# Pairs of expert blocks by seven block products in the second half of a dense expert sum

## The chip, the cores and the metric

The kernel runs on one core of a Trainium2 chip. Its time is the device time of one launch in microseconds (us), the median of several runs. PE is TensorE, DVE is VectorE, ACT is ScalarE, POOL is GpSimd, SP is SyncE.

## What is computed

Two transformer blocks, one behind the other, on 256 tokens of width 2048, in float32. The change is in the last stage of the second block, the expert layer:

```
        expert = jnp.take_along_axis(cand_i, pos, axis=-1)
        g = jax.nn.softmax(top_s, axis=-1)
        u = u_emb[expert]
        a = jax.nn.gelu(jnp.einsum('thkd,td->thk', u, xb).astype(jnp.float32), approximate=False)
        coef = (g * a).astype(xb.dtype)
        return jnp.einsum('thk,thkd->td', coef, v_emb[expert])
```

There are 128 x 128 experts. A token chooses 128 of them (8 heads, 16 each). The result is added to the residual and normalised.

## The kernel before

The expert layer is computed densely. A stage U multiplies all 16384 rows of `peer_u` with the tokens, and a gate table, zero where a token did not choose an expert, makes the coefficients `G[:, j, :]` (128 experts of block j by 256 tokens). Stage V is one product: coefficients, transposed, times `peer_v`, summed over 128 blocks j. It goes in two halves of the output's columns: for c = 0 all blocks j and columns 0 to 1023, then for c = 1 all blocks j and columns 1024 to 2047. `PLAN` lists these tiles in order; tile ("V", j, c) is a load of 128 x 1024 (512 KB) and 12 matmuls.

Every float32 product is made of three matmuls (`three`, lines 940 to 943): high by high, high by low and low by high. The high part of an operand is a copy rounded by ACT, the low part is a subtraction on DVE (raw minus high). So each tile needs: the load into `raw` (SP's queue, four buffers, line 842; it waits for the low part of the tile four before), ACT's `cut` (line 2273, three buffers `wh`), DVE's `cut` (line 1481, into `wl`), and the coefficients' high part on ACT (`coef_high`, line 2655) and low part on DVE (`coef_low`, line 2189), two buffers. In the iteration of tile j, ACT and DVE make the coefficients of tile j + 1 and cut the weights of the tile two further on. Both wait, through ACT, for the end of tile j - 1 on PE. PE (`v_tile`) waits for the low weights and the low coefficients of its tile, and adds into four PSUM banks (two of 128 tokens by two of 512 columns) over all j. Each engine has its own list of instructions, in the order in which the code is written, and runs it in that order; between engines there are semaphores only.

Columns 0 to 1023 stay in PSUM banks 4 to 7 until they are added to the residual, which comes back from memory (`PIECE`, line 918) into `fin` and is summed, squared and scaled at tiles 50 to 64 (`ADD_AT`). The last tiles and the end of the norm stand behind. GpSimd does nothing in this stage; its sums of 128x256 and 128x258 in earlier stages are at lines 2721 and 2759.

## Time and profile before

| | |
|---|---|
| median of 3 runs | 3175.16 us (3174.51 to 3175.98) |
| profiled execution | 3175.95 us, its span 3174.1 us |
| busy share of the span | PE 100%, PE's weight loads 95%, DVE 66%, ACT 57%, POOL 14% |
| traffic | 627.77 MB, mean 198 GB/s |

Busy time counts from an instruction's start to its end. Matmuls are pipelined and overlap, so the duration of one is more than what it adds to the time. An instruction on DVE or ACT can also start a little before the one ahead has ended.

### The profile page before, as it was taken

To read this page: it belongs to the slowest core of one execution; us is meant where nothing else is said; L and a number is where in the kernel's file an instruction comes from. 1 tells how busy PE (TensorE), PEld (TensorE's weight loads), DVE (VectorE), ACT (ScalarE), POOL (GpSimd) and SP (SyncE) were. 2 spreads that over 40 slices of the span, in tenths; PEclk is the share of its full clock that TensorE was granted. 3 is DMA by queue.
4 is the path that set the end of the run, shared out by engine and by line. 5 is a ranking of instruction groups with operands and counts; after the bars stand their busy time and mean duration, and the time that the engine had idled before them with its cause. 6 is when DMAs were issued, how large, how long until landed. Compare 5 with 4: busy or idle time off the path is not lost.

```text
span 3174.1 us, 58774 instructions
## 1 busy us (share of the span) xinstructions
PE 3160.3 (100%) x24186; PEld 3018.3 (95%) x24186; DVE 2096.0 (66%) x3389; ACT 1804.0 (57%) x2580; POOL 458.0 (14%) x321
## 2 busy tenths in 40 slices
PE   9999999999999999999999999999999999999998
PEld 9999999999999999999999999999999888888887
DVE  7987486666664477665666699855555666666665
ACT  6566464444444455545455578877777544555545
POOL 0001200000000000000000056777760000000000
PEclk9999999999999999999999999999999999999999
DMA  6444557666666656545565577888876777766555
GB/s 224 151 146 134 183 181 235 225 226 229 226 201 194 194 172 206 163 153 166 187 196 197 199 190 194 196 195 195 194 195 196 243 242 242 242 226 216 195 194 168
DMA packets 229419, 627.77 MB, mean 198 GB/s; under 512 B 59328, under 2 KB 78624, under 8 KB 229024
## 3 DMA queue, kind: packets, MB, share of 16 engines
q1 hardware_dynamic: 192144, 623.60, 60.7%
q0 software_dynamic: 36864, 0.15, 3.3%
q8 instruction: 192, 3.15, 0.4%
q14 instruction: 75, 0.61, 0.1%
q10 hardware_dynamic: 144, 0.26, 0.0%
HBM read 601.27 MB, written 21.10 MB: 196 GB/s over the span
## 4 chain that ended last, share of the span: by engine, by line
PE 98%; DVE 1%; ACT 0%; DMA 0%; issue 0%; POOL 0%; SPq 0%; DVEq 0%; ACTq 0%; POOLq 0%
PE ps L941 32%; PE ps L942 31%; PE ps L943 31%; PE ps L1014 0%; DVE wl L1481 0%; PE ps L1215 0%; PE ps L1238 0%; PE ps L1235 0%; PE ps L982 0%; DMA raw<-in_in1k 0%; PE ps L1411 0%; PE ps L1249 0%; PE ps L1239 0%; PE ps L1067 0%; PE ps L1016 0%
## 5 line engine op out<-in xcount | busy, mean ns | idle before, releaser
L2273 ACT CAST wh<-raw 128x1024 fp32r<-128x1024 f32 (+3 forms) x1114 | 1158.2, 1040 | 1029.7 <-PE ps L943 1008.4
L1481 DVE TENSOR_TENSOR wl<-raw,wh 128x1024 fp32r<-128x1024 f32 (+2 forms) x883 | 1061.8, 1203 | 407.8 <-ACT wh L2273 405.4
L941 PE MATMUL ps<-xh,wh 128*128 128x256 f32 x3088 | 854.7, 277 | 0.5 <-issue 0.5
L943 PE MATMUL ps<-xh,wl 128*128 128x256 f32 x3088 | 850.0, 275 | 0.0
L942 PE MATMUL ps<-xl,wh 128*128 128x256 f32 x3088 | 849.8, 275 | 0.0
L941 PE MATMUL ps<-xw,wh 128*128 128x258 f32 (+2 forms) x2096 | 591.7, 282 | 2.8 <-DVE wl L1542 1.7
L943 PE MATMUL ps<-xw,wl 128*128 128x258 f32 (+2 forms) x2096 | 587.6, 280 | 0.0
L941 PEld LDWEIGHTS ps<-xh,wh 128*128 128x128 f32 x3088 | 579.7, 188 | 4.3 <-issue 1.6
L942 PEld LDWEIGHTS ps<-xl,wh 128*128 128x128 f32 x3088 | 579.8, 188 | 1.1 <-issue 1.0
L943 PEld LDWEIGHTS ps<-xh,wl 128*128 128x128 f32 x3088 | 579.6, 188 | 0.0
L2784 POOL DMA_INDIRECT table<-w_loose x256 | 397.6, 1553 | 809.3 <-DVE w_loose L2161 656.3
L1481 DVE TENSOR_TENSOR wl<-raw,ph 128x1024 fp32r<-128x1024 f32 x231 | 281.2, 1220 | 224.4 <-ACT ph L2278 187.7
L942 PE MATMUL ps<-xw,wh 128*128 128x258 f32 (+2 forms) x1441 | 404.2, 281 | 0.0
L941 PEld LDWEIGHTS ps<-xw,wh 128*128 128x128 f32 x2096 | 394.3, 188 | 5.4 <-DVE wl L1542 2.1
L943 PE MATMUL ps<-wh,coefs 128*128 128x512 f32 x1020 | 396.8, 389 | 0.0
L941 PE MATMUL ps<-wh,coefs 128*128 128x512 f32 x1020 | 396.8, 389 | 0.0
L942 PE MATMUL ps<-wl,coefs 128*128 128x512 f32 x1020 | 396.8, 389 | 0.0
L943 PEld LDWEIGHTS ps<-xw,wl 128*128 128x128 f32 x2096 | 394.0, 188 | 0.0
L942 PEld LDWEIGHTS ps<-xw,wh 128*128 128x128 f32 x1441 | 270.8, 188 | 0.1
L2278 ACT CAST ph<-raw 128x1024 fp32r<-128x1024 f32 x231 | 232.7, 1007 | 0.0
L941 PEld LDWEIGHTS ps<-wh,coefs 128*128 128x128 f32 x1020 | 191.4, 188 | 39.8
L943 PEld LDWEIGHTS ps<-wh,coefs 128*128 128x128 f32 x1020 | 191.4, 188 | 39.8
(398 smaller groups left out, 4454.7 us busy)
## 6 DMA issues: line engine op xcount, KB each, us to landing
raw<-in_peer_u SPq DMA_DIRECT2D x256, 512.0 KB
raw<-in_peer_v SPq DMA_DIRECT2D x256, 512.0 KB
...
```

The lines of the kernel that those rows point to most:

```text
L941: t.matmul(o, lh, rh, start=start, stop=False)
L942: t.matmul(o, lh, rl, start=False, stop=False)
L943: return t.matmul(o, ll, rh, start=False, stop=stop)
L1481: v.tensor_tensor(part_at(wl, i), raw[:, i % RN, 0:cols(i)], high.bitcast(F32), ALU.subtract).then_inc(lo, 1)
L2273: last = s.copy(part_at(wh, i), raw[:, i % RN, 0:cols(i)])
L2278: last = s.copy(ph[:, 2 + i % 2, :], raw[:, i % RN, 0:cols(i)])
L2784: g.indirect_dma_start(out=table, out_offset=bass.IndirectOffsetOnAxis(ap=eidx[q][:, n:n + 1], axis=0), in_=wts[q][:, n:n + 1], in_offset= ...
```

## The change

In the second half (c = 1), eleven pairs of neighbouring blocks (26 and 27, 34 and 35, ... 106 and 107) leave the plan of tiles. A pair is a 2 x 2 by 2 x 2 block product: coefficients of two blocks for two groups of tokens, times weights of two blocks for two groups of columns. Eight block products of three matmuls (24) become seven (21), in the manner of Strassen and Winograd: some factors are sums of blocks, and the results go to the four banks of this half and to four more, which collect over all pairs and are folded in once behind the last.

A pair's rows are loaded apart, into columns of `G` that are no longer needed. GpSimd makes four sums of 128x512 (weights) and four of 128x128 (coefficients) in the six tiles between two pairs (`pair_sums`). ACT makes the high parts (`pair_step` of the scalar part) and DVE the low parts (`pair_low_of`) in five steps of 512, 1024, 1024, 1024 and 512 columns, one to a tile (`BEHIND_PAIR`); the low part is written over the raw sum. PE (`v_pair`) computes the pair ahead of tile j + 2. The load of the next pair stands in SP's queue ahead of a tile's load and waits for DVE's second step and GpSimd's fourth sum of the pair before, which are the last readers of these rows. The residual's first half is added at tiles 11 to 14, as banks 4 to 7 are wanted by the pairs. The lines left out of the diff write `fin` as a function `fin_at` with another layout, and fold the extra banks in (`fold`, eight sums at tiles 109 to 116).

```diff
@@ -158,7 +158,10 @@
 PLAN += [("out2", m, c) for m in range(16) for c in range(2)]
 PLAN += [("wq", m, c) for m in range(8) for c in range(2)]
 PLAN += [("U", j, c) for j in range(128) for c in range(2)]
-PLAN += [("V", j, c) for c in range(2) for j in range(128)]
+PAIRS = [26 + 8 * n for n in range(11)]
+PAIRED = [j + e for j in PAIRS for e in range(2)]
+SINGLE = [j for j in range(128) if j not in PAIRED]
+PLAN += [("V", j, 0) for j in range(128)] + [("V", j, 1) for j in SINGLE]
 AT = {key: i for i, key in enumerate(PLAN)}
 NCH = len(PLAN)
 I1, O1, GU, DN = AT["in1k", 0, 0], AT["out1", 0, 0], AT["guk", 0, 0], AT["down", 0, 0]
@@ -166,9 +169,17 @@
 I2, BA, O2, WQ, U0 = AT["in2k", 0, 0], AT["ba", 0, 0], AT["out2", 0, 0], AT["wq", 0, 0], AT["U", 0, 0]
 V1 = AT["V", 0, 1]
 
-PIECE = {AT["V", 10 + 2 * n, 1]: n for n in range(12)}
-
-ADD_AT = [50 + 4 * n for n in range(4)]
+PIECE = {AT["V", j, 1]: n for n, j in enumerate((8, 10, 12, 14, 109, 110, 111, 112, 28, 30, 32, 33))}
+
+ADD_AT = [11, 12, 13, 14]
+SQUARE_AT, GAIN_AT = [113, 114, 115, 116], [117, 118, 119, 120]
+
+
+BETWEEN = PAIRS[1] - PAIRS[0] - 2
+PAIR_LOAD = {AT["V", 20, 1]: 0}
+PAIR_LOAD.update({AT["V", j - BETWEEN, 1] + 9: n + 1 for n, j in enumerate(PAIRS[:-1])})
+BEHIND_PAIR = {j - BETWEEN + o: (n, o) for n, j in enumerate(PAIRS) for o in range(BETWEEN)}
+FOLD = {PAIRS[-1] + 3 + n: n for n in range(8)}
 UEND = [AT["U", j, 1] - U0 for j in range(128)]
 UAT = {slot + 1: j for j, slot in enumerate(UEND)}
 
...
+    def fin_at(qt, c, n=512):
+        o = 2 * CH * (c // CH) + CH * qt + c % CH
+        return flatG[:, o:o + n]
+
+    pair_high, pair_low = [x[:, PAD_X[3]:PAD_X[3] + KT * S] for x in xbuf]
+    pair_raw = x_loose[:, 1, PAD_X[3]:PAD_X[3] + KT * S]
+    B11, B21, B22, T1_, T3_, T2_, T4_, SUMS = range(8)
...
+    RAW11, RAW12, RAW21, RAW22 = [flatG[:, 2 * CH + 512 * n:2 * CH + 512 * n + 512] for n in range(4)]
+    RAW_ROWS = flatG[:, 3 * CH:4 * CH]
+    folded = flatG[:, 3 * D + 3 * CH:3 * D + 3 * CH + 512]
...
@@ -914,10 +943,24 @@
                     y.wait_ge(d_spill, 16)
                 y.wait_ge(c_l, 128 + 2 * n + 2)
                 c = slice(512 * (n % 4), 512 * (n % 4) + 512)
+                if n == 4:
+                    y.wait_ge(pair_lo, PAIR_LO + 5 * (len(PAIRS) - 1) + 2)
+                    y.wait_ge(pair_sum, PAIR_SUM + 8 * (len(PAIRS) - 1) + 4)
                 if n < 8:
-                    y.dma_start(fin[:, n // 4, c], spill[:, n // 4, c]).then_inc(d_re, 16)
+                    qt, x = n // 2 % 2, CH * (n // 4) + 512 * (n % 2)
+                    y.dma_start(fin_at(qt, x), spill[:, qt, x:x + 512]).then_inc(d_re if n < 4 else d_gf, 16)
                 else:
                     y.dma_start(gain[:, c], A["g_final"][:, c]).then_inc(d_gf, 16)
+            if i in PAIR_LOAD:
+                n = PAIR_LOAD[i]
+                if n:
+                    y.wait_ge(pair_lo, PAIR_LO + 5 * (n - 1) + 2)
+                    y.wait_ge(pair_sum, PAIR_SUM + 8 * (n - 1) + 4)
+                else:
+                    y.wait_ge(c_l, 128 + 16)
+                for e in range(2):
+                    j = PAIRS[n] + e
+                    y.dma_start(flatG[:, (2 + e) * CH:(3 + e) * CH], A["peer_v_2"][128 * j:128 * j + 128, CH:2 * CH]).then_inc(d_pair, 16)
             load(i)
             if 0 <= i - I2 - 6 < len(SIDES2):
                 for name, a in SIDES2[i - I2 - 6]:
@@ -1433,6 +1476,34 @@
                 last = v_part_of(j, half, a)
             last.then_inc(gemm, 1)
 
+        def v_pair(n):
+            j = PAIRS[n]
+            one, two = 128 + j, 128 + j + 1
+            first, last = n == 0, n == len(PAIRS) - 1
+
+            def product(o, left, b, start, stop):
+                return three(o[:], *left, pair_block(pair_high, b), pair_block(pair_low, b), start, stop)
+
+            def single(tile, qt):
+                tk = slice(128 * qt, 128 * qt + 128)
+                return coef_at(0, tile)[:, tk], coef_at(1, tile)[:, tk]
+
+            def summed(i):
+                return pair_sum_at(pair_high, i), pair_sum_at(pair_low, i)
+
+            if first:
+                t.wait_ge(f_add, 4)
+            t.wait_ge(pair_lo, PAIR_LO + 5 * (n + 1))
+            t.wait_ge(c_l, one + 1)
+            product(ps[4], single(one, 0), B11, first, last)
+            product(ps[5], summed(0), T1_, first, last)
+            t.wait_ge(c_l, two + 1)
+            product(acc(1, 0, 0), single(two, 0), B21, False, False)
+            product(acc(1, 1, 0), single(two, 1), T4_, False, False).then_inc(pair_mm, 1)
+            product(acc(1, 0, 1), summed(3), B22, False, False)
+            product(ps[6], summed(1), T2_, first, last)
+            product(ps[7], summed(2), T3_, first, last).then_inc(pair_mm, 1)
+
         def v_last():
 
             for j in range(125, 128):
@@ -1462,6 +1533,8 @@
             elif (j, c) == (125, 1):
                 v_last()
             elif c == 0 or j < 125:
+                if c and j - 2 in PAIRS:
+                    v_pair(PAIRS.index(j - 2))
                 v_tile(j, c)
             if i < V1:
                 for step, a in SIDES3[i - U0]:
...
+            x = fin_at(qt, 512 * i)
             v.tensor_tensor(x, x, acc(half, qt, b)[:], ALU.add).then_inc(f_add, 1)
 
+        def pair_step(n, o):
+            if 1 <= o < 6:
+                pair_low_of(n, o - 1)
+
+        def pair_low_of(n, q):
+            x, y = ((0, 512), (512, 1536), (1536, 2560), (2560, 3584), (3584, 4096))[q]
+            whole_ = RAW11 if q == 0 else RAW_ROWS if q == 1 else pair_raw[:, x:y]
+            v.wait_ge(pair_hi, PAIR_HI + 5 * n + q + 1)
+            v.tensor_tensor(pair_low[:, x:y], whole_, pair_high[:, x:y].bitcast(F32), ALU.subtract).then_inc(pair_lo, 1)
+
+        def fold(n):
+
+            steps = [(folded, ps[4]), (fin_at(0, CH + 512), folded), (fin_at(0, CH + 512), ps[5]), (folded, ps[7]),
+                     (fin_at(1, CH), folded), (fin_at(1, CH + 512), folded), (fin_at(1, CH + 512), ps[5]), (fin_at(0, CH), ps[4])]
+            x, y = steps[n]
+            if n == 0:
+                v.wait_ge(pair_hi, PAIR_HI + 5 * len(PAIRS) + 1)
+                v.wait_ge(d_gf, 16 * 8)
+            else:
+                v.wait_ge(pair_sum, PAIR_SUM + 8 * len(PAIRS) + n)
...
+            v.tensor_tensor(x, x, y if y is folded else y[:], ALU.add).then_inc(pair_sum, 1)
+
         for j in range(128):
+            if j in PAIRS:
+                coef_low(128 + j + 1)
+                cut(AT["V", j + 2, 1] + 2)
+                continue
             if j < 125:
                 coef_low(128 + j + 1)
             if j == 124:
@@ -2220,18 +2319,22 @@
                     last = v.tensor_tensor(part_at(wl, NCH - 1)[:, c], raw[:, (NCH - 1) % RN, c],
                                            part_at(wh, NCH - 1)[:, c].bitcast(F32), ALU.subtract)
                 last.then_inc(lo, 1)
-            else:
-                cut(V1 + j + 2)
+            elif j in SINGLE and j - 2 not in PAIRS:
+                cut(AT["V", j, 1] + 2)
+            if j in BEHIND_PAIR:
+                pair_step(*BEHIND_PAIR[j])
+            if j in FOLD:
+                fold(FOLD[j])
             if j in ADD_AT:
                 n = ADD_AT.index(j)
                 if n == 0:
-                    v.wait_ge(d_re, 16 * 8)
...
@@ -2648,6 +2751,8 @@
             j = n % 128
             if n == 255:
                 s.wait_ge(gemm, AT["U", 127, 1] + 1)
+            elif n >= 130 and n - 130 in PAIRED:
+                s.wait_ge(pair_mm, PAIR_MM + 2 * (PAIRED.index(n - 130) // 2) + 1)
             elif n >= 2:
                 s.wait_ge(gemm, AT["V", (n - 2) % 128, (n - 2) // 128] + 1)
+            s.activation(squares[:, qt, 512 * i:512 * i + 512], fin_at(qt, 512 * i), ACT.Square,
                          accum_out=ssum[:, qt, i:i + 1]).then_inc(f_sq, 1)
 
+        def pair_step(n, o):
+            if o > 4:
+                return
+            x, y = ((0, 512), (512, 1536), (1536, 2560), (2560, 3584), (3584, 4096))[o]
+            whole_ = RAW11 if o == 0 else RAW_ROWS if o == 1 else pair_raw[:, x:y]
+            if o == 0:
+                if n:
+                    s.wait_ge(pair_mm, PAIR_MM + 2 * n)
+                s.wait_ge(d_pair, D_PAIR + 32 * (n + 1))
+            elif o > 1:
+                s.wait_ge(pair_sum, PAIR_SUM + 8 * n + (3, 4, 8)[o - 2])
+            s.copy(pair_high[:, x:y], whole_).then_inc(pair_hi, 1)
+
         for j in range(128):
+            if j in PAIRS:
+                coef_high(128 + j + 1)
+                cut(AT["V", j + 2, 1] + 2)
+                continue
             if j < 126:
                 coef_high(128 + j + 1)
             if j == 124:
@@ -2682,10 +2804,15 @@
                 s.wait_ge(gemm, i - SN + 1)
                 s.copy(part_at(wh, i)[:, 0:512], raw[:, i % RN, 0:512]).then_inc(hi_front, 1)
                 s.copy(part_at(wh, i)[:, 512:CH], raw[:, i % RN, 512:CH]).then_inc(hi, 1)
-            else:
+            elif j in SINGLE and j - 2 not in PAIRS:
                 cut(AT["V", j, 1] + 2)
-            if j - 1 in ADD_AT:
-                n = ADD_AT.index(j - 1)
+            if j in BEHIND_PAIR:
+                pair_step(*BEHIND_PAIR[j])
+            if j == PAIRS[-1] + 2:
+                s.wait_ge(pair_mm, PAIR_MM + 2 * len(PAIRS))
+                s.copy(folded, ps[6][:]).then_inc(pair_hi, 1)
+            if j in SQUARE_AT:
+                n = SQUARE_AT.index(j)
                 square_up(0, n // 2, n % 2)
         for qt in range(2):
...
+
+        def pair_sums(n):
+            j = PAIRS[n]
+            g.wait_ge(coef, j + 2)
+            g.wait_ge(c_l, 128 + 16)
+            a11, a21, a12, a22 = [G[:, j + e, 128 * qt:128 * qt + 128] for e in range(2) for qt in range(2)]
+            t1, t2, t3, t4 = [pair_block(pair_raw, b) for b in (T1_, T2_, T3_, T4_)]
+            sums = [pair_sum_at(pair_raw, i) for i in range(4)]
+            done = PAIR_SUM + 8 * n
+            if n:
+                g.wait_ge(pair_mm, PAIR_MM + 2 * n)
+            g.wait_ge(d_pair, D_PAIR + 32 * (n + 1))
+            g.tensor_tensor(t1, RAW12, RAW11, ALU.subtract).then_inc(pair_sum, 1)
+            g.tensor_tensor(t3, RAW22, RAW12, ALU.subtract).then_inc(pair_sum, 1)
+            g.wait_ge(pair_sum, done + 1)
+            g.tensor_tensor(t2, RAW22, t1, ALU.subtract).then_inc(pair_sum, 1)
+            g.wait_ge(pair_sum, done + 3)
+            g.tensor_tensor(t4, RAW21, t2, ALU.subtract).then_inc(pair_sum, 1)
+            g.tensor_tensor(sums[0], a21, a22, ALU.add).then_inc(pair_sum, 1)
+            g.tensor_tensor(sums[2], a11, a21, ALU.subtract).then_inc(pair_sum, 1)
+            g.wait_ge(pair_sum, done + 5)
+            g.tensor_tensor(sums[1], sums[0], a11, ALU.subtract).then_inc(pair_sum, 1)
+            g.wait_ge(pair_sum, done + 7)
+            g.tensor_tensor(sums[3], a12, sums[1], ALU.subtract).then_inc(pair_sum, 1)
+
+        for n in range(len(PAIRS)):
+            pair_sums(n)
 
     px.close()
     top.close()
```

How the instructions stand now. On DVE, in the second half of V before, two kinds of rows alternate from tile to tile (`coefs` is `coef_low`, `wl` the cut of the weights):

```order
L2189 TENSOR_TENSOR coefs<-G,coefs 128x256
L1481 TENSOR_TENSOR wl<-raw,wh 128x1024
L2189 TENSOR_TENSOR coefs<-G,coefs 128x256
L1481 TENSOR_TENSOR wl<-raw,wh 128x1024
L2189 TENSOR_TENSOR coefs<-G,coefs 128x256
```

In the changed kernel the same place, from the last four steps ahead of one pair to the first cut behind it (`xl` is the pair's low part, L2262 is `coef_low` and L1554 the cut):

```order
L2290 TENSOR_TENSOR xl<-x_loose,xh 128x1024
L2262 TENSOR_TENSOR coefs<-G,coefs 128x256
L1554 TENSOR_TENSOR wl<-raw,wh 128x1024
L2290 TENSOR_TENSOR xl<-x_loose,xh 128x512
L2262 TENSOR_TENSOR coefs<-G,coefs 128x256
L1554 TENSOR_TENSOR wl<-raw,wh 128x1024
L2262 TENSOR_TENSOR coefs<-G,coefs 128x256 x3
L1554 TENSOR_TENSOR wl<-raw,wh 128x1024
```

Each tile between two pairs has a third instruction behind its cut, and the pair's last piece (512 columns) stands behind the cut of a tile that comes after the pair. On GpSimd, which had no row in this stage, one pair's sums read (`x_loose` is the pair's raw buffer):

```order
L2945 TENSOR_TENSOR x_loose<-G 128x512
L2946 TENSOR_TENSOR x_loose<-G 128x512
L2948 TENSOR_TENSOR x_loose<-G,x_loose 128x512
L2950 TENSOR_TENSOR x_loose<-G,x_loose 128x512
L2951 TENSOR_TENSOR x_loose<-G 128x128
L2952 TENSOR_TENSOR x_loose<-G 128x128
L2954 TENSOR_TENSOR x_loose<-x_loose,G 128x128
L2956 TENSOR_TENSOR x_loose<-G,x_loose 128x128
```

Both inputs of every one lie in SBUF, as do both inputs of DVE's coefficients, cuts and pieces.

## Rows read from the trace of the kernel before

**Rows 1.** The page: busy us (share) x instructions; granted clock in tenths, 40 slices.

```profile
PE 3160.3 (100%) x24186; PEld 3018.3 (95%) x24186; DVE 2096.0 (66%) x3389; ACT 1804.0 (57%) x2580; POOL 458.0 (14%) x321
...
PEclk9999999999999999999999999999999999999999
```

**Rows 2.** The page: the chain that ended last, by engine.

```profile
PE 98%; DVE 1%; ACT 0%; DMA 0%; issue 0%; POOL 0%; SPq 0%; DVEq 0%; ACTq 0%; POOLq 0%
```

**Rows 3.** Windows of V, halves 1 and 2: busy us, clock, DMA share, GB/s.

```profile
2500.00:2600.00 100.00, 100.00 (x443) 82.81 (x442) 69.54 (x110) 49.55 (x74) 0.00 (x0) 1.00 0.75 241
...
2810.00:3155.00 345.00, 345.00 (x1524) 285.67 (x1523) 213.81 (x263) 175.01 (x263) 0.00 (x0) 1.00 0.62 201
```

**Rows 4.** Timeline, second half of V: start, us, engine, line [idle before].

```profile
2901.74 0.39 PE L941 MATMUL ps<-wh,coefs 128*128 128x512 f32 x1
...
2901.94 0.41 ACT L2655 CAST coefs<-G 128x256 fp32r<-128x256 f32 x1 [1.36 <-PE ps L943]
...
2902.25 1.05 ACT L2273 CAST wh<-raw 128x1024 fp32r<-128x1024 f32 x1
2902.38 0.43 DVE L2189 TENSOR_TENSOR coefs<-G,coefs 128x256 fp32r<-128x256 f32 x1 [0.54 <-ACT coefs L2655]
...
2903.34 1.23 DVE L1481 TENSOR_TENSOR wl<-raw,wh 128x1024 fp32r<-128x1024 f32 x1 [0.53 <-ACT wh L2273]
...
2904.46 0.39 PE L941 MATMUL ps<-wh,coefs 128*128 128x512 f32 x1
```

**Rows 5.** Timeline, DVE: two cuts back to back, merged.

```profile
932.82 2.35 DVE L1481 TENSOR_TENSOR wl<-raw,wh 128x1024 fp32r<-128x1024 f32 x2
```

**Rows 6.** Groups by form: busy us, mean ns of one.

```profile
L1481 DVE TENSOR_TENSOR wl<-raw,wh 128x512 fp32r<-128x512 f32 x16 | 11.1, 693 | 17.0 <-ACT wh L2273 17.0
...
L1835 DVE SCALAR_TENSOR_TENSOR snt<-mt,snt 128x768 f32<-128x768 f32 x1 | 1.0, 954 | 0.0
...
L2273 ACT CAST wh<-raw 128x512 fp32r<-128x512 f32 x16 | 10.0, 622 | 26.6 <-PE ps L943 26.6
```

**Rows 7.** Timeline at the start: PE released by DVE.

```profile
9.30 0.69 DVE L1542 TENSOR_TENSOR wl<-raw,wh 128x512 fp32r<-128x512 f32 x1 [1.73 <-ACT wh L2315]
...
10.04 0.39 PE L941 MATMUL ps<-xw,wh 128*128 128x272 f32 x1 [1.20 <-DVE wl L1542]
...
10.27 0.28 PE L942 MATMUL ps<-xw,wh 128*128 128x272 f32 x1
```

**Rows 8.** Timeline: a GpSimd sum just ahead of a DVE instruction.

```profile
931.34 0.74 POOL L2721 TENSOR_TENSOR tmp<-tmp 128x256 f32<-128x256 f32 x1 [481.18 <-ACT tmp L2437]
...
931.38 1.52 DVE L1833 SCALAR_TENSOR_TENSOR snt<-mt 128x768 f32<-128x768 f32 x1
```

**Rows 9.** Timeline: a GpSimd sum issued during a cut on DVE.

```profile
946.29 1.22 DVE L1481 TENSOR_TENSOR wl<-raw,wh 128x1024 fp32r<-128x1024 f32 x1 [0.46 <-ACT wh L2273]
...
946.62 1.50 POOL L2721 TENSOR_TENSOR tmp<-tmp 128x256 f32<-128x256 f32 x1 [14.53 <-ACT tmp L2437]
```

**Rows 10.** Groups by form, POOL: fills of one and of 1024 columns.

```profile
L2763 POOL MEMSET tmp<- 128x1024 f32 x1 | 1.0, 956 | 49.6 <-DVE rstd L1515 49.6
...
L2917 POOL MEMSET const-uint8-127<- 128x1 uint8 x1 | 0.1, 129 | 0.0
```

**Rows 11.** DMA issues: KB each, median us from issue to landing.

```profile
spill<-G SPq DMA_DIRECT2D x1, 2048.0 KB, 7.8
G<-spill SPq DMA_DIRECT2D x8, 256.0 KB, 5.2
```

**Rows 12.** Timelines of DVE and POOL: a GpSimd sum across a boundary on DVE.

```profile
114.74 1.21 DVE L1481 TENSOR_TENSOR wl<-raw,wh 128x1024 fp32r<-128x1024 f32 x1
115.87 0.71 DVE L1648 SCALAR_TENSOR_TENSOR pexp<-pexp,stat 16x16 f32<-16x16 f32 x1
...
114.90 1.65 POOL L2759 TENSOR_TENSOR csum<-cacc 128x258 f32<-128x258 f32 x1 [88.48 <-DVE cacc L1692]
...
272.57 1.22 DVE L1481 TENSOR_TENSOR wl<-raw,wh 128x1024 fp32r<-128x1024 f32 x1
...
272.34 2.06 POOL L2759 TENSOR_TENSOR csum<-csum,cacc 128x258 f32<-128x258 f32 x1 [62.96 <-DVE cacc L1692]
```

More of the change, by code:

```diff
@@ L933, in _ @@
                     y.wait_ge(sem, 2 * qt + n + 1)
-                    y.dma_start(out[128 * qt:128 * qt + 128, c:c + 512], fin[:, qt, c:c + 512]).then_inc(d_out, 16)
+                    y.dma_start(out[128 * qt:128 * qt + 128, c:c + 512], fin_at(qt, c)).then_inc(d_out, 16)
         y.wait_ge(d_out, 8 * 16)
@@ L2670, in square_up @@
             s.wait_ge(f_add, n + 1)
-            s.activation(squares[:, qt, 512 * i:512 * i + 512], fin[:, qt, 512 * i:512 * i + 512], ACT.Square,
+            s.activation(squares[:, qt, 512 * i:512 * i + 512], fin_at(qt, 512 * i), ACT.Square,
                          accum_out=ssum[:, qt, i:i + 1]).then_inc(f_sq, 1)
+        def pair_step(n, o):
[10 more added lines that the diff above has]
+            s.copy(pair_high[:, x:y], whole_).then_inc(pair_hi, 1)
         for j in range(128):
+            if j in PAIRS:
+                coef_high(128 + j + 1)
+                cut(AT["V", j + 2, 1] + 2)
+                continue
             if j < 126:
@@ L2697, in _ @@
                     s.wait_ge(f_add, 8 + n)
-                    s.activation(squares[:, 1, c:c + 256], fin[:, 1, c:c + 256], ACT.Square,
+                    s.activation(squares[:, 1, c:c + 256], fin_at(1, c, 256), ACT.Square,
                                  accum_out=ssum[:, 1, 3 + n:4 + n]).then_inc(f_sq, 1)
@@ L2704, in _ @@
             for c in (0, 512):
-                x = fin[:, qt, c:c + 512]
+                x = fin_at(qt, c)
                 s.activation(x, x, ACT.Copy, scale=r).then_inc(f_out, 1)
@@ L2708, in _ @@
                 s.wait_ge(f_out, 4)
-                s.dma_start(out[128:256, 512:1024], fin[:, 1, 512:1024]).then_inc(d_out, 16)
+                s.dma_start(out[128:256, 512:1024], fin_at(1, 512)).then_inc(d_out, 16)
     @block.gpsimd
```

19 lines of the change are left out of this document (12 added, 7 removed).

## The prediction

> **What bounds the kernel now.** I read the busy shares first: PE is busy for the whole span, at the full clock, and POOL has almost nothing to do [rows 1]. The chain of waits says the same from the other end: 98% of it is PE [rows 2]. For the stretch that the change touches, the second half of V, the windows give PE 345.00 busy of 345.00 us, with DVE at 62% and ACT at 51% [rows 3]. So here time is matmuls times their pitch, plus whatever a change makes PE wait. In the timeline one tile's first matmul starts at 2901.74 and the next tile's at 2904.46, 2.72 us later: 12 matmuls, 0.2267 us each [rows 4]. Their own 0.39 us overlap, so that figure is not the price.
>
> The same rows give the rhythm of the helpers, which I count from a tile's first matmul T (2901.74). ACT gets word that the tile before is done at T+0.20 and makes the high coefficients, then the high half of the weights; DVE starts its low coefficients at T+0.64 and its low weights at T+1.60, ending at T+2.83 [rows 4]. Back to back a DVE instruction costs less than its duration, as each starts before the last has ended: two cuts of 1024 take 2.35 us, so 1.13 apiece where one lasts 1.22 [rows 5]. Taking the same 0.09 off, 256 columns cost 0.34, and a cut of 512, which lasts 0.69 (ACT's 0.62), costs 0.60 [rows 6].
>
> **What the change removes.** A pair has 7 products of 3 matmuls in place of two tiles with 12 each: 21 for 24. Eleven pairs drop 33 matmuls, all 512 wide: 33 x 0.2267 = 7.5 us. Nothing else on PE goes away. That is 0.24% of 3175.16, hardly more than the 0.2% that a measurement of this kernel tells from no change, so the waits decide.
>
> **What it adds on DVE and ACT.** Per period of eight tiles two cuts go and 4096 columns of high and low parts come: on DVE 2 x 1.13 less, 0.60 + 3 x 1.13 + 0.60 = 4.59 more. Averages are fine (about 14 us of DVE in 21 us), but the place is not. All of the 4.59 stands in the five tiles ahead of the pair, and the last piece stands behind a cut that cannot come earlier. I set 0 at the first matmul of tile 28, the first behind a pair, and walk DVE to the next pair (34, 35), due at 6 x 2.72 = 16.32:
> - tile 29 (2.72): coefficients 3.36 to 3.70, cut at 4.32 to 5.45, first piece to 6.05
> - tile 30 (5.44): coefficients 6.08 to 6.42, cut at 7.04 to 8.17, second piece to 9.30
> - tile 31: coefficients to 9.64, cut 9.76 to 10.89, third piece to 12.02
> - tile 32: coefficients to 12.36, cut 12.48 to 13.61, fourth piece to 14.74
> - tile 33 (13.60): coefficients to 15.08, cut waits for ACT until 15.20, to 16.33, last piece ends at 16.33 + 0.69 = 17.02.
>
> PE waits for all five pieces before the pair's first product. It is 0.70 late; a stalled PE starts 0.05 after the release, and its second matmul comes 0.23 behind the first, where at 272 columns 0.12 is the pitch (0.2267 x 272 / 512) [rows 7], so each pair costs about 0.85 us. The last cut is for the second tile behind the pair and nobody needs it yet, but it stands ahead of the piece that is needed. Eleven times 0.85 is 9.4 us: with GpSimd costing nothing the sum is already -7.5 + 9.4 = +1.9 us, 3177. ACT (0.41 + 1.05 + 1.05 = 2.5 a tile) fits in 2.72.
>
> **What GpSimd's sums cost.** They are on no chain by themselves, but they read SBUF while DVE does. A 128x256 sum took 0.74 us beside a DVE instruction that came just after it, and that DVE instruction took 1.52 [rows 8], where its like of the same size takes 0.954 [rows 6]: DVE was held 0.57 us, to 0.61 after the sum's start. The other way round, a sum issued 0.33 after a cut took 1.50 and ended 0.61 after the cut [rows 9]. So the two exclude each other, with 0.13 us of dispatch ahead and about 0.48 in which DVE is held. No 512-wide sum is in this trace. Below, the slope of the fills, (956 - 129) / 1023 = 0.81 ns a column, makes it 0.61 + 0.21 = 0.82; above, twice the whole, 1.48 with dispatch. I take 0.10 to 0.13 as fixed, from the one-column fill [rows 10], which leaves 2.0 ns a column, nearest to the sum's own row: 1.12 for 512 (0.99 of it holding DVE), 0.35 for 128 (0.22 holding).
>
> The eight sums start at 0.2, when the pair before has finished. Two of 512 are over before DVE's first work at 3.36. The third, from about 3.1, holds DVE 0.75, the fourth 1.0, the four small ones 0.2 each: 2.55 in all. DVE's waits for ACT in the walk above (0.62 + 0.03 + 0.62 + 3 x 0.12 = 1.63) absorb that much; 0.9 is left. Behind the first pair, whose sums run before DVE is loaded, a pair costs 0.85 + 0.9 = 1.75. Together 0.85 + 10 x 1.75 = 18.4, less 7.5: **+10.9 us, 3186**. The profiled execution took 3175.95, its span 3174.1; both stand within 1 us of the median, so the difference goes on either.
>
> The Trainium skill (SBUF — State Buffer, "Who interferes with whom") has it harder: a DVE instruction with two SBUF inputs and a GpSimd one that reads SBUF exclude each other for the whole instruction. The exclusion agrees with the trace [rows 8, 9]; that DVE was let go 0.13 us before the sum's end does not. By the whole instruction the blocks would be 0.9 + 1.12 + 4 x 0.35 = 3.4 a period, 1.8 left, 2.65 a pair, and the sum +19.9 (3195). The row decides, but it is of 256 columns, so 3195 lies in my range. The same skill (GPSIMD Engine Reference, "Elementwise — side-by-side cycle accounting") gives 4497 ns for such a sum of 2048 columns; no run here shows it, and an estimate between it and the 0.74 row is 1.28 for 512 with dispatch, which would leave the sum where it is.
>
> **What costs nothing.** SP's queue now waits at each pair's loads for DVE's second piece (about 9.3 to 11.4) and the fourth sum (6.8). Behind it stand the loads of tiles 31 and on in the next period, whose first reader comes some 14 us later; the pair's own 1 MB is read at 23.5. Landing took 5.2 us for 256 KB and 7.8 for 2 MB [rows 11], so 12 us cover it. The bytes are the same in nearly the same time, 201 GB/s, and the first half of V ran at 241 without a wait of PE [rows 3]. If the cover went, each late load would stall the pair by what it is late. The added sums at tiles 11 to 14, the eight folds at 109 to 116 (0.68 each behind 0.34 + 1.13, so 2.15 of 2.72) and the squares on ACT fit in their tiles, and the tail after the last matmul is the same instructions.
>
> **The rivals.**
> - *The sums find gaps and DVE loses nothing* (the sums shorter than I take them, below 1.0 us for 512): +2 to +6, 3177 to 3181. For it: DVE pauses four times in a period. Against: DVE is nearly full from 9.30 on. 0.20.
> - *DVE keeps the port from one instruction to the next*, and the sums get in only when it pauses. The rows speak both ways: a sum issued at 114.90 got in at the end of the running cut, and a 16x16 instruction issued behind it took 0.71; one issued at 272.34 ended 2.06 later, 0.61 after a cut that started at 272.57, so it missed the boundary at 272.66 [rows 12]. Behind the last sum stand ACT's 0.62, then coefficients and a cut on ACT (1.4) and coefficients, cut and piece on DVE (0.34 + 1.13 + 0.69), about 4.4 us. It bites once the last sum ends later than 11.9; near 15.8 it makes each later pair 3.9 late: 0.85 + 39 - 7.5 = +32, 3207. 0.13.
> - *Faster*: the pair starts unhindered. The one place is the last piece: if it ended by 16.3 at every pair, the 7.5 us would stand, 3167.7. It needs the last cut to be 0.7 us shorter or earlier, and the rows fix all its terms [rows 4 to 6]; it decides below 0.1 us of stall a pair. 0.04.
> - *Stalls bring PE's clock down* from 2.4 to 1.2 GHz, of which no row of V shows anything (granted 1.00, also at the start with 1.2 us stalls). Then a stretch behind each pair would cost double, far over 3207. 0.02.
>
> **How the numbers follow.** My forecast (+7 to +22, with the alternation of DVE and GpSimd) has 0.61, 3182 to 3197 by itself. The range runs from the floor, 3177, to 3206, which leaves out the faster case, the clock and part of the port rival: about 0.17. The same case below +6.3 us: 0.20. Faster 0.04. Slower 0.76.
>
> **What would show it.** PE's busy time loses 7.5 us of matmul while the span grows; waits of PE's first product of a pair on DVE's low pieces, eleven, the first near 0.8 and the others near 1.7; DVE's coefficients and pieces with 0.2 to 1.0 us added while a GpSimd sum of 512 runs, and none of the 4.6 us of pieces missing. Granted clock 1.00. I am wrong if the pieces are over before the pair is due, if the waits fall on loads, or if the sums leave DVE's durations alone.

## The result: 3195.8 us, 0.65% slower

After the change the kernel takes 3195.81 us (median; 3195.35 to 3196.55, 4 runs) beside 3175.11 of the kernel before: a ratio of 1.0065, 95% interval 1.0053 to 1.0078. The profiled execution has a span of 3194.7 us, 20.6 more than before. Slower was the likeliest case and the time lies in the range, but the size is nearly twice the +10.9 us that the prediction had. One execution of the kernel of experiment 12 went at a granted clock of 0.83 and took 3558.41 us; it is left out, and all others used here went at 0.998 or more. The page of after, beside [rows 1, 2]: busy us and share of each engine, the granted clock in tenths, and the chain of waits by engine.

```profile
PE 3167.6 (99%) x24153; PEld 3012.0 (94%) x24153; DVE 2147.8 (67%) x3430; ACT 1825.9 (57%) x2614; POOL 560.7 (18%) x409
...
PEclk9999999999999999999999999999999999999999
...
PE 93%; DVE 6%; ACT 1%; DMA 0%; issue 0%; POOL 0%; SPq 0%; DVEq 0%; ACTq 0%; POOLq 0%
```

The prediction wanted PE's busy time to lose 7.5 us. 33 matmuls are gone, and yet it gained 7.3. The waits (engine, line, releaser: us in total, times, longest) show stalls on both of DVE's products:

```profile
PE ps L984 <- DVE xl L2290: 11.5, 10, 2.3
...
PE ps L984 <- DVE coefs L2262: 0.8, 3, 0.4
```

A wait that the profile puts down to nobody is missing there, so I measured stalls by the starts of neighbouring matmuls instead. After's timeline in one period: DVE and POOL behind a pair, then the next pair's start (start, us, engine, line).

```profile
2920.76 1.30 POOL L2948 TENSOR_TENSOR x_loose<-G,x_loose 128x512 f32<-128x512 f32 x1
2921.30 1.04 DVE L2262 TENSOR_TENSOR coefs<-G,coefs 128x256 fp32r<-128x256 f32 x1 [4.12 <-ACT coefs L2760]
2922.14 1.36 POOL L2950 TENSOR_TENSOR x_loose<-G,x_loose 128x512 f32<-128x512 f32 x1
2922.27 2.32 DVE L1554 TENSOR_TENSOR wl<-raw,wh 128x1024 fp32r<-128x1024 f32 x1
...
2934.33 1.21 DVE L1554 TENSOR_TENSOR wl<-raw,wh 128x1024 fp32r<-128x1024 f32 x1
...
2934.78 0.39 PE L986 MATMUL ps<-wh,coefs 128*128 128x512 f32 x1
...
2935.47 0.68 DVE L2290 TENSOR_TENSOR xl<-x_loose,xh 128x512 fp32r<-128x512 f32 x1
...
2936.20 0.49 PE L984 MATMUL ps<-xh,coefs 128*128 128x512 f32 x1 [1.03 <-DVE xl L2290]
2936.54 0.39 PE L985 MATMUL ps<-xl,coefs 128*128 128x512 f32 x1
```

Both mechanisms of the forecast are there. The last piece stands behind a cut and releases PE at 2936.15 (2935.47 + 0.68); 1.42 us lie between the pair's first matmul and the one before it, and 0.34 behind it. And a cut that takes 1.22 alone took 2.32, since GpSimd's fourth sum ran until 2923.50: the cut ended 1.09 us later, so DVE was let go 0.13 before the sum's end. The same 0.13 comes out at the coefficients (1.04 for 0.41, 0.28 after the third sum's end at 2922.06).

What was not foreseen is between the stalls. In this piece of after nothing waits; the first row and the one 12 matmuls behind it:

```profile
2999.83 0.40 PE L986 MATMUL ps<-wh,coefs 128*128 128x512 f32 x1
...
3002.63 0.40 PE L986 MATMUL ps<-wh,coefs 128*128 128x512 f32 x1
```

That is 2.80 us for 12, 0.2333 apiece, where before has 2.72 and 0.2267 [rows 4], with the granted clock at 1.00 in both. I call this distance from one matmul's start to the next one's the pitch. From the first stall (2868.35) up to 3150 us, after has 72 stretches of 13 gaps in which nothing stalls: 68 go at 0.2333 and 4 lie between the two values; in before, all 95 such stretches go at 0.2267. There are some 1,140 gaps between 2868.35 and 3154, and what they take above 0.2267, stalls apart, is 7.3 us.

The second surprise is at the last pair. ScalarE waits for two tiles that SP's queue issued late: in front of them, at the first of the residual's late pieces (line 948), the queue itself had waited 14.0 us. PE stalls 2.4 us, and the granted clock falls. The wait of SP's queue (engine, line, releaser: us in total, times, longest):

```profile
SPq L948 <- DVE xl L2290: 14.0, 1, 14.0
```

After's timeline, ScalarE and PE:

```profile
3120.98 1.05 ACT L2376 CAST wh<-raw 128x1024 fp32r<-128x1024 f32 x1 [1.64 <-DMA raw<-in_peer_v]
...
3123.94 0.79 PE L984 MATMUL ps<-xh,coefs 128*128 128x512 f32 x1 [2.25 <-DVE xl L2290]
3124.53 0.63 PE L985 MATMUL ps<-xl,coefs 128*128 128x512 f32 x1
3124.96 0.63 PE L986 MATMUL ps<-xh,coefs 128*128 128x512 f32 x1
```

The matmuls behind the wait are 0.43 us apart. The windows of after for that stretch (us; busy of PE, PEld, DVE, ACT, POOL with their counts; clock, DMA share, GB/s) have the clock at 0.52, most of the time at the lower of its two levels:

```profile
3123.50:3127.00 3.50, 3.06 (x7) 2.48 (x8) 1.95 (x3) 1.04 (x1) 0.00 (x0) 0.52 1.02 397
```

The sum of after, from its own timeline: the gaps between matmuls, each less 0.2333, come to 20.55 us (first pair with the tiles ahead of it 1.5, nine regular pairs at 1.63 = 14.7, last pair 4.3), plus 7.3 for the pitch, less 7.5: +20.4, where 20.6 was measured.

### The profile page after: what moved, and what is told of

Its sections match the earlier page's. It is cut to its first block, busy times and chain, and to the rows that moved or that the text cites. A ratio compares the mean times of both kernels' runs of the same rounds, so it can differ in the third digit from the quotient of the medians.

```text
span 3194.7 us, 58881 instructions
## 1 busy us (share of the span) xinstructions
PE 3167.6 (99%) x24153; PEld 3012.0 (94%) x24153; DVE 2147.8 (67%) x3430; ACT 1825.9 (57%) x2614; POOL 560.7 (18%) x409
## 4 chain that ended last, share of the span: by engine, by line
PE 93%; DVE 6%; ACT 1%; DMA 0%; issue 0%; POOL 0%; SPq 0%; DVEq 0%; ACTq 0%; POOLq 0%
PE ps L984 30%; PE ps L985 30%; PE ps L986 30%; DVE wl L1554 2%; DVE xl L2290 2%; DVE coefs L2262 1%; PE ps L1057 0%; PE ps L1258 0%; PE ps L1278 0%; PE ps L1281 0%; PE ps L1025 0%; PE ps L1454 0%; PE ps L1292 0%; PE ps L1282 0%; DMA raw<-in_peer_v 0%
## 5 line engine op out<-in xcount | busy, mean ns | idle before, releaser
L2376 ACT CAST wh<-raw 128x1024 fp32r<-128x1024 f32 (+3 forms) x1092 | 1134.8, 1039 | 1032.2 <-PE ps L986 1009.5
L1554 DVE TENSOR_TENSOR wl<-raw,wh 128x1024 fp32r<-128x1024 f32 (+2 forms) x861 | 1050.4, 1221 | 364.4 <-ACT wh L2376 360.5
L1554 DVE TENSOR_TENSOR wl<-raw,ph 128x1024 fp32r<-128x1024 f32 x231 | 281.2, 1220 | 224.0 <-ACT ph L2381 203.0
L984 PE MATMUL ps<-wh,coefs 128*128 128x512 f32 x932 | 366.0, 393 | 1.7 <-DVE coefs L2262 0.8
L985 PE MATMUL ps<-wl,coefs 128*128 128x512 f32 x932 | 364.6, 391 | 0.0
L986 PE MATMUL ps<-wh,coefs 128*128 128x512 f32 x932 | 364.5, 391 | 0.0
L2262 DVE TENSOR_TENSOR coefs<-G,coefs 128x256 fp32r<-128x256 f32 x254 | 118.0, 468 | 183.5 <-ACT coefs L2760 183.2
L984 PEld LDWEIGHTS ps<-wh,coefs 128*128 128x128 f32 x932 | 175.1, 188 | 44.8 <-issue 8.1
```

The costliest lines, as they stand in the source:

```text
L984: t.matmul(o, lh, rh, start=start, stop=False)
L985: t.matmul(o, lh, rl, start=False, stop=False)
L986: return t.matmul(o, ll, rh, start=False, stop=stop)
L1554: v.tensor_tensor(part_at(wl, i), raw[:, i % RN, 0:cols(i)], high.bitcast(F32), ALU.subtract).then_inc(lo, 1)
L2262: v.tensor_tensor(coef_at(1, n), G[:, n % 128, :], coef_at(0, n).bitcast(F32), ALU.subtract).then_inc(c_l, 1)
L2376: last = s.copy(part_at(wh, i), raw[:, i % RN, 0:cols(i)])
```

## The experiments

Twelve kernels, each timed beside the kernel before (3175.3 to 3175.6 us on those chips). Times are medians; "stalls" are the gaps between matmuls summed as above, and "stretches" are 13 gaps without a stall, from 2868 to 3150 us.

**1. One short wait in the kernel before.** Nothing of the change is in it.

```diff
             t.wait_ge(c_l, n + 1)
+            if n == 128 + 20:
+                t.wait_ge(lo, AT["V", 21, 1] + 1)
```

> The kernel before with one extra wait: PE starts tile 20 of the second half only when the low weights of tile 21 are done, which stalls it once, by about 0.2 us. Theory (a stall of PE in V leaves the matmul pitch at 0.2333 us instead of 0.2267 for all that follows): 108 tiles x 12 x 0.0066 = 8.5 us more, about 3184. Rival (the longer pitch comes from the pairs, from GpSimd or from the other work): 0.2 us more, 3175.3, pitch 0.2267 to the end.

3183.96 us, ratio 1.0028 [1.0018, 1.0038]. Its timeline around the wait:

```profile
2869.16 0.39 PE L942 MATMUL ps<-wl,coefs 128*128 128x512 f32 x1
...
2870.52 0.39 PE L942 MATMUL ps<-wl,coefs 128*128 128x512 f32 x1
2870.74 0.39 PE L943 MATMUL ps<-wh,coefs 128*128 128x512 f32 x1
2871.22 0.47 PE L941 MATMUL ps<-wh,coefs 128*128 128x512 f32 x1
2871.52 0.40 PE L942 MATMUL ps<-wl,coefs 128*128 128x512 f32 x1
...
2874.32 0.40 PE L942 MATMUL ps<-wl,coefs 128*128 128x512 f32 x1
```

From 2869.16 to 2870.52 there are 6 matmuls, 0.2267 apiece; 0.48 and 0.30 at it, a stall of 0.3 us; then 2871.52 to 2874.32 for 12, and so to the end. A stall of 0.3 us cost 8.7: the time moved as the theory had it, and not by the rival's 0.2.

**2 to 4. The parts of the stalls.** Run 2 puts fills of the same places for GpSimd's sums (its result and run 4's lack them); run 3 puts DVE's last piece ahead of the cut; run 4 does both.

```diff
-            g.tensor_tensor(t1, RAW12, RAW11, ALU.subtract).then_inc(pair_sum, 1)
+            g.memset(t1, 0.0).then_inc(pair_sum, 1)
...
             elif j in SINGLE and j - 2 not in PAIRS:
+                if BEHIND_PAIR.get(j, (0, 0))[1] == 5:
+                    pair_step(*BEHIND_PAIR[j])
                 cut(AT["V", j, 1] + 2)
```

> The changed kernel with GpSimd's eight sums a pair replaced by fills of the same tiles with zero (the sums are left out): the same order and semaphores, but nothing is read. Theory (a sum that reads SBUF holds DVE, and DVE it): DVE's coefficients, cuts and pieces keep 0.42, 1.22 and 0.69, each pair waits 0.85 instead of 1.65, so about 8 us less, 3188. Rival (GpSimd's sums are too slow or the held DVE does not matter): 3195 to 3196.

> The changed kernel with DVE's last piece of a pair ahead of the cut of the tile behind the pair instead of behind it. Theory (the place behind that cut is 1.1 us of each pair's wait): the wait falls from about 1.2 to 0.1 to 0.2 us at eleven pairs, some 11 us less, 3184 to 3185. Rival (the cut becomes late instead): a wait of the same size on the low weights, 3195.

> Both at once: fills in place of sums (sums left out) and the last piece first. Theory (the stalls, and the pitch that they leave behind, are all that stands against the 33 matmuls): no wait of PE between the pairs, pitch 0.2267 to the end, 3175.1 - 7.5 = 3167.7. Rival (pairs cost something by themselves, or the pitch changes without a stall): 3176 or more.

Run 2: 3184.06, ratio 1.0028 [1.0017, 1.0039]; stalls 9.1 us. A cut's mean is 1226 ns again (after: 1421), PE's waits for the pieces are half, and a pair costs 0.78 us where the walk had 0.85. Grouped by line between 2870 and 3150 us, after and then run 2:

```profile
L1554 DVE TENSOR_TENSOR wl<-raw,wh 128x1024 fp32r<-128x1024 f32 x75 | 106.5, 1421 | 8.0 <-ACT wh L2376 6.6
```

```profile
L1554 DVE TENSOR_TENSOR wl<-raw,wh 128x1024 fp32r<-128x1024 f32 x79 | 96.9, 1226 | 29.2 <-ACT wh L2376 26.2
```

Run 2's waits of PE, for the 11.5 of after:

```profile
PE ps L984 <- DVE xl L2290: 5.6, 10, 1.0
```

Run 3: 3182.58, ratio 1.0022 [1.0013, 1.0032]; stalls 7.1 us, 3.9 of them now at a tile's coefficients, 0.3 and more apiece, and 3.2 at the pairs. Either edit takes 12 to 13 us off after, more than the 8 and 11 expected: the 20.55 us of stalls fell by 11.4 and 13.4, the long last one among them. Run 4: 3175.50, ratio 1.0001 [0.9991, 1.0010]. It stalls nowhere, no weights load of PE comes late at the first pair or ahead of it, and its pitch still goes to 0.2333 at the first pair. I had expected 3167.7. So a stall is not the only thing that changes the pitch.

**5. The late residual.** SP's queue asks for the second half's residual behind tiles 111 to 114 instead of 109 to 112; folds and gains move back with it.

```diff
-PIECE = {... (8, 10, 12, 14, 109, 110, 111, 112, 28, 30, 32, 33))}
+PIECE = {... (8, 10, 12, 14, 111, 112, 113, 114, 28, 30, 32, 33))}
-FOLD = {PAIRS[-1] + 3 + n: n for n in range(8)}
+FOLD = {PAIRS[-1] + 6 + n: n for n in range(8)}
```

> After's kernel with the four late residual pieces asked for behind tiles 111 to 114 instead of 109 to 112, and the folds three tiles and the gains three tiles later. In after's trace ScalarE waits 1.64 and 1.56 us for a raw tile just ahead of the last pair, the pair is 2.6 us late instead of 1.4, and the granted clock is 0.5 for 3.4 us behind it. Theory (the residual pieces' waits at the head of SP's queue delay the loads of tiles 109 and 110): ScalarE's two waits are gone, the last pair stalls like the others, the clock stays at 1.00, and the time is 2.7 to 3 us below after's, about 3193. Rival (the last pair is late for another reason): still 3195.8 with the low clock.

3193.48, ratio 1.0057 [1.0040, 1.0074]: 2.3 us below after, where 2.7 to 3 were expected; stalls 17.5. ScalarE's waits for raw tiles and the queue's 14.0 us are gone, the last pair stalls like the others, and the clock is 1.00 in the windows:

```profile
3100.00:3130.00 30.00, 28.86 (x124) 22.71 (x123) 18.14 (x22) 14.30 (x23) 9.37 (x8) 1.00 0.54 172
```

**6. The pair's places in SBUF.** Run 4 again (and again without the sums), with the pair's blocks moved by 28 words.

```diff
-    pair_high, pair_low = [x[:, PAD_X[3]:PAD_X[3] + KT * S] for x in xbuf]
+    pair_high, pair_low = [x[:, 0:KT * S + 4] for x in xbuf]
...
-        return x[:, 512 * SUMS + 128 * n:512 * SUMS + 128 * n + 128]
+        return x[:, 512 * SUMS + 4 + 128 * n:512 * SUMS + 4 + 128 * n + 128]
```

> The fourth experiment again (GpSimd fills the sums' places with zeros in place of computing them, so the output lacks the sums; DVE's last piece ahead of the cut), with the pair's blocks moved by 28 words: they begin where a multiple of 64 words begins, as V's tiles do, and the sums at 4 words past one, as the coefficients do. Theory (the pitch of the 512-wide matmuls depends on where the two operands lie relative to each other, and the pair's other alignment shifted it): no pair leaves another alignment behind, the pitch stays at 0.2267 us, and the time is 8 us below the fourth experiment's, 3167 to 3168. Rival (it is something else in the pair, its order of PSUM banks or the weights' changes, that brings 0.2333): 3175.5 again, with 0.2333 from the first pair on.

3169.81 (3167.91 to 3170.30, 10 runs; run 4's ten lie between 3174.64 and 3175.98), ratio 0.9982 [0.9972, 0.9991]. The same 24 us in the windows of run 4 and of this one; the number behind PE's busy time counts its matmuls, 105 and 108:

```profile
3013.00:3037.00 24.00, 24.00 (x105) 19.41 (x104) 17.13 (x23) 14.23 (x22) 2.62 (x8) 1.00 0.64 201
```

```profile
3013.00:3037.00 24.00, 24.00 (x108) 19.87 (x106) 17.21 (x22) 14.22 (x21) 2.62 (x8) 1.00 0.60 212
```

Only the places differ, so in run 4 they brought the other pitch. The trace is of the fastest execution, 3167.91 us, which keeps 0.2267 through every pair although it has small stalls at 3099 and 3103 us (0.6), where raw tiles are late. The other nine took 3169.3 to 3170.3 and have no trace. A stall there that brings 0.2333 would cost them some 220 matmuls x 0.0066 = 1.5 us, by estimate; that this is the difference is not shown.

**7. Everything real together:** runs 3, 5 and 6 with the sums.

> After's full computation with three edits: DVE's last piece ahead of the cut (third experiment), the late residual (this call's first) and the moved blocks (this call's second). The stalls of the third experiment remain (0.3 us at a coefficient, 0.2 us at a pair), and one stall is enough for 0.2333 us. Theory: the moved blocks bring nothing as long as anything stalls; 3182.6 less up to 1 us for the last pair, 3181 to 3183. Rival (with the same alignment everywhere a stall leaves the pitch at 0.2267): 3174 to 3175.

3181.90, ratio 1.0020 [1.0010, 1.0029]; stalls 7.1. But its pitch is not 0.2333 throughout: 14 of 64 stretches go at 0.2267. It changes both ways, each time where PE's weights load (PEld in a timeline) starts late. On time it starts with the matmul ahead of its own, within 0.01 us. The first change needs no gap between matmuls: the load at 2868.95 comes 0.11 late, its matmul is on time, and from the next one on the distance is 0.2333:

```profile
2868.84 0.39 PE L986 MATMUL ps<-wh,coefs 128*128 128x512 f32 x1
2868.95 0.19 PEld L984 LDWEIGHTS ps<-wh,coefs 128*128 128x128 f32 x1 [0.15 <-issue]
2869.06 0.39 PE L984 MATMUL ps<-wh,coefs 128*128 128x512 f32 x1
...
2869.53 0.40 PE L986 MATMUL ps<-wh,coefs 128*128 128x512 f32 x1
```

Here is a change for the worse at a stall, at 2924:

```profile
2922.84 0.39 PE L985 MATMUL ps<-wl,coefs 128*128 128x512 f32 x1
2923.06 0.39 PE L986 MATMUL ps<-wh,coefs 128*128 128x512 f32 x1
2923.29 0.39 PE L984 MATMUL ps<-wh,coefs 128*128 128x512 f32 x1
...
2924.14 0.47 PE L984 MATMUL ps<-wh,coefs 128*128 128x512 f32 x1
...
2924.68 0.40 PE L986 MATMUL ps<-wh,coefs 128*128 128x512 f32 x1
2924.91 0.39 PE L984 MATMUL ps<-wh,coefs 128*128 128x512 f32 x1
2925.14 0.39 PE L985 MATMUL ps<-wl,coefs 128*128 128x512 f32 x1
```

**8. The sums on DVE.** Run 7, with the eight sums taken from GpSimd: in the tile behind a pair, where DVE has no cut, and the two tiles after it.

```diff
+            if o == 0:
+                step(0, t1, RAW12, RAW11, ALU.subtract)
+                step(0, t3, RAW22, RAW12, ALU.subtract)
+                pair_low_of(n, 0)
+                step(1, t2, RAW22, t1, ALU.subtract)
+            elif o == 1:
+                step(3, t4, RAW21, t2, ALU.subtract)
...
-        for n in range(len(PAIRS)):
-            pair_sums(n)
```

> As the one before, but the eight sums of a pair are on DVE instead of GpSimd: three 512-wide ones and the first low piece in the tile behind the pair, which has no cut, the rest in the next two tiles. In a period of 21.1 us of matmuls DVE has some 15.2 us of its own work; GpSimd's sums, during which DVE starts nothing, are 7.2 more, 22.4 in all, more than the period has; on DVE they are 4 x 0.69 + 4 x 0.25 = 3.8, 19.0 in all. Theory (the stalls come from DVE plus GpSimd filling the period): no stall that repeats, PE at one matmul behind the other, and with the pitch at 0.2267 3167.7, with 0.2333 3175 to 3176. Rival (it is the order of the pieces and not the sum that stalls): stalls of 0.3 to 1 us at each pair, 3178 to 3184.

3176.68, ratio 1.0004 [0.9994, 1.0014]. Stalls fall from 7.1 to 0.6 us, all five before 2890, and the pitch is 0.2333 from the first of them (2876.26) to the end. So the repeating stalls came from DVE filled with its own work and held by GpSimd's.

**9. The first pair's sums two tiles earlier,** from tile 18 on.

> The kernel with the sums on DVE, with the first pair's sums begun two tiles earlier, at tile 18, so that they spread over the tiles, which all have a cut there. In the run before, DVE's four long instructions behind tile 20 made the coefficients of tile 22 0.26 us late and the first pair 0.1, and from that first stall on every matmul came 0.2333 us behind the one before; nothing stalled afterwards. Theory (one stall decides the pitch for all that follows, and with the moved blocks the pairs themselves don't): no stall, 0.2267 to the end, 3167 to 3169. Rival (the pitch is lost for another reason, the pairs' own for one): no stall, but 0.2333 from the first pair on, 3175 to 3176.

3175.50, ratio 0.9998 [0.9989, 1.0007]. No gap above 0.255 us is left, and the pitch still changes, at 2887.39. DVE's last piece, the matmuls and the pair's weights load there:

```profile
2886.68 0.69 DVE L2327 TENSOR_TENSOR xl<-x_loose,xh 128x512 fp32r<-128x512 f32 x1
...
2887.16 0.39 PE L985 MATMUL ps<-wl,coefs 128*128 128x512 f32 x1
...
2887.39 0.40 PE L986 MATMUL ps<-wh,coefs 128*128 128x512 f32 x1
2887.44 0.19 PEld L984 LDWEIGHTS ps<-xh,coefs 128*128 128x128 f32 x1
2887.63 0.39 PE L984 MATMUL ps<-xh,coefs 128*128 128x512 f32 x1
```

The piece ended at 2887.37, and the pair's weights load was due with the matmul at 2887.39. It started at 2887.44, 0.05 us late; no other load between 2801 and that matmul is late, and the pitch changes there. In run 6 the margin at the first pair was 0.32 us (a piece's end at 2886.39, the load due at 2886.71), and the pitch stayed. The expected time was missed, and the question was whether such a hair is enough (run 12).

**10. The coefficients moved by 4 words,** in the kernel before: both operands of V then begin at the same place of 64.

```diff
-    ... for o in (4, 580)]
+    ... for o in (0, 576)]
```

> The kernel before, and in it both halves of the coefficients' buffer begin at word 0 of 64 instead of word 4; V's weights then begin where its moving tiles do. Nothing stalls. Theory (the pitch goes with the relative place of the two operands): the pitch of V's 3,072 512-wide matmuls changes; if 4 words are what makes 0.2267, all or part of them take 0.2333, up to 3072 x 0.0066 = 20 us more, 3195. Rival (only a stall or the pair's mixed places change it): 3175.3, pitch 0.2267.

3175.47, ratio 1.0000 [0.9990, 1.0009], 0.2267 in all 95 stretches. The rival was right: a distance of 0 or 4 words between the two operands makes no difference to the pitch.

**11. Nine waits in the kernel before,** at tiles 20, 30, ... 100.

```diff
+            if n in range(128 + 20, 128 + 110, 10):
+                t.wait_ge(lo, AT["V", n - 127, 1] + 1)
```

> The kernel before with the first experiment's wait at nine tiles, 20 to 100 by tens, instead of one. Each costs some 0.3 us, 2.7 in all. Theory A (after a stall the pitch is 0.2333 for good): 3175.3 + 8.5 + 2.7 = 3186.5, with 0.2333 everywhere from tile 20 on. Theory B (each stall lets the pitch fall to one of its two values anew, as the combined kernel's trace has it, where it goes back to 0.2267 at 2912 and 2957 us): stretches of both, and a time between 3178 and 3186.5. Rival C (a stall costs its own length alone): 3178.

3183.95, ratio 1.0027 [1.0016, 1.0038]: theory B. (The traced execution took 3182.43, the lowest of seven; the highest took 3185.81.) Its windows between the waits (24 us each):

```profile
2958.00:2982.00 24.00, 24.00 (x104) 19.48 (x103) 16.63 (x22) 13.28 (x22) 0.00 (x0) 1.00 0.54 180
3013.00:3037.00 24.00, 24.00 (x107) 19.88 (x107) 14.45 (x17) 11.51 (x19) 0.00 (x0) 1.00 0.60 196
3041.00:3065.00 24.00, 24.00 (x104) 19.45 (x104) 14.12 (x17) 11.04 (x17) 0.00 (x0) 1.00 0.57 190
3070.00:3094.00 24.00, 24.00 (x104) 19.48 (x103) 13.87 (x18) 11.79 (x18) 0.00 (x0) 1.00 0.56 181
3098.00:3122.00 24.00, 24.00 (x108) 19.88 (x107) 14.14 (x19) 12.23 (x18) 0.00 (x0) 1.00 0.56 188
```

The sixth wait brings 0.2267 back, the seventh takes it, the ninth brings it back; between waits nothing changes. All with one kind of operands and the clock at 1.00. After two of the nine waits it is 0.2267.

**12. Two cuts behind the pieces.** Run 9 with the cuts of a pair's last two tiles done one tile later, behind the last low piece.

```diff
             if j in PAIRS:
                 coef_low(128 + j + 1)
+                cut(AT["V", j - 1, 1] + 2)
                 cut(AT["V", j + 2, 1] + 2)
...
                 if BEHIND_PAIR.get(j, (0, 0))[1] == 5:
                     pair_step(*BEHIND_PAIR[j])
-                cut(AT["V", j, 1] + 2)
+                    cut(AT["V", j - 1, 1] + 2)
+                elif BEHIND_PAIR.get(j, (0, 0))[1] != 4:
+                    cut(AT["V", j, 1] + 2)
```

> The kernel of the eleventh run with two of a pair's DVE cuts moved behind the pair's last low piece: the cut of the tile before the last is done in the last one's turn, that one's in the pair's. In the run before, nothing stalled by more than 0.02 us, but DVE ended the first pair's last low piece at 2887.37 us, where the pair's first matmul, to be on time, had its weights called for at about 2887.4, and the pitch went to 0.2333 from the matmul before on; in the eighth run, where the same piece ended at 2886.40 for a start at 2886.72, the pitch stayed at 0.2267 through every pair. Theory (a hair's wait at a pair is enough to change the pitch): the pieces end 1 us earlier, no pair waits, 0.2267 to the end, 3167.5 to 3169. Rival (sums on DVE, or another thing that the eighth run left out, brings 0.2333 by itself): 3175.5 again, from 2887 us on.

(That text calls run 9 the eleventh and run 6 the eighth.)

3167.93 (median of ten, 3167.19 to 3169.71), ratio 0.9977 [0.9968, 0.9986]: 0.23% below the kernel before, with the full computation. The page of run 12:

```profile
PE 3152.3 (100%) x24153; PEld 3011.7 (95%) x24153; DVE 2153.4 (68%) x3518; ACT 1826.1 (58%) x2614; POOL 458.6 (14%) x321
```

Its timeline at the first pair, DVE's last piece, the pair's weights load and its first matmul:

```profile
2886.37 0.69 DVE L2327 TENSOR_TENSOR xl<-x_loose,xh 128x512 fp32r<-128x512 f32 x1
...
2887.89 0.19 PEld L984 LDWEIGHTS ps<-xh,coefs 128*128 128x128 f32 x1
2888.11 0.39 PE L984 MATMUL ps<-xh,coefs 128*128 128x512 f32 x1
```

And one of its windows, to be read beside run 11's:

```profile
3041.00:3065.00 24.00, 24.00 (x108) 19.88 (x107) 20.35 (x32) 13.67 (x22) 0.00 (x0) 1.00 0.59 200
```

The piece ends 1.05 us ahead of the pair's first matmul, 0.83 ahead of its weights load, and so at all eleven pairs (run 9: 0.02 ahead of the load's due time at the first pair, 0.33 at the others). No weights load is late up to 3150 us, and the pitch is 0.2267 in all 95 stretches. The first late load comes at 3151.09, by 0.05 us, and the pitch changes there. PE's busy time is 8.0 us below before's, the 7.5 of the 33 matmuls and little else.

## Why the prediction was right, and where not

- *PE bounds the kernel; 33 matmuls are worth 7.5 us*: right. Run 12 shows the gain bare (-7.5 us by the medians).
- *The last piece behind the cut, 0.85 us a pair*: right; 0.78 measured without the sums (run 2). The walk holds with the pitch that was there: 1.60 + 1.13 + 0.69 behind tile 33's start are 0.62 more than a tile of 2.80 us, and 0.05 and 0.1 come on top as forecast.
- *GpSimd's sums, 0.9 a pair*: the total is right; 1.63 less 0.78 is 0.85. Its place is not: 0.35 of the 1.63 falls two tiles ahead of the pair, at a tile's low coefficients, which the walk never let be late, and 1.28 at the pair, where 1.7 was forecast. And it is partly luck: a 512-wide sum took 1.29 us or more and not 1.12, and a 128-wide one waits for DVE (1.45, mean, for the first of them); against that stands the slack that the slower pitch gave DVE, 6 x 0.08 us a period. That the two cancel is my estimate and was not run. The Trainium skill (GPSIMD Engine Reference, "Elementwise — side-by-side cycle accounting") gave 1.28 by the estimate, and was the closer; the prediction took it to leave the sum where it is, but put into its own working it adds 0.16 for each of the two sums that hold DVE. The rule of the Trainium skill (SBUF — State Buffer, "Who interferes with whom"), an exclusion for the whole instruction, holds to 0.13 us: DVE was let go that much before the sum's end, as [rows 8] had it. The 3195 that the prediction worked out from a hold of the whole instruction meets 3195.8 by accident: it has 2.65 us a pair, where 1.63 was measured, and no change of pitch.
- *"Time is matmuls times their pitch, plus whatever a change makes PE wait"*: here is the step that failed. The pitch was taken as a constant, from a trace in which nothing stalls. It has two values, a stall sets it anew, and 7.3 us of the 9.8 between 3186 and 3195.8 are that; 2.2 are stalls beyond the 18.4 forecast. Runs 1, 11 and 12 show it from three sides. That the time still lies in the range is luck: the range was wide for the price of GpSimd's sums, and what filled it was the pitch, which no term and no rival named.
- *"What costs nothing": the residual's pieces on SP's queue*: wrong, by 2.3 to 3 us (run 5). I had the bytes and not the waits: the first of the four waits for the last pair's second low piece and fourth sum, 14.0 us on the queue, and stands ahead of tile 109's load.
- *The first pair* costs 1.5 with the tiles ahead of it, where 0.85 stood; its sums hold DVE ahead of the first pair (low coefficients of 256 columns that end at 2869.02 took 1.51 us).
- *The rivals*: "the sums find gaps" and "DVE keeps the port" did not come; DVE and GpSimd alternate. Of "PE's clock drops", the 1.2 GHz level appears once in V, behind a stall of 2.4 us, for about 3.5 us. "Faster" needed the last piece in time at every pair; runs 4 and 9 stalled nowhere and gained nothing, because of the pitch.

**Open.** What the pitch hangs on. Shown: a weights load that comes 0.05 us or more late lets it be set anew, to either value, more often 0.2333, with a stall between matmuls (runs 1, 7, 11) or without one (0.11 late in run 7, 0.05 in run 9 and, at 3151 us, in run 12); between late loads it stays in runs 7, 9, 11 and 12; the pair's operands at 28 words changed it without a late load in run 4, and at 0 not in runs 6 and 12. That it is a matter of how the two streams of SBUF reads meet is only argued, and run 10 speaks against the simplest form. That the late load in run 9 is what changed it rests on its row, on its like in run 7, and on run 12, which moved two cuts a pair and nothing else; the moved cuts also change when DVE reads, and that was not tested apart. Run 12 with the old places wasn't tried, so what the moved places and the late residual are worth in it is not known.
